# Scores on 128 contraction rows and five single-column fp32 products in a two-block transformer kernel

## The reference

```
block 1: h = rms_norm(x);  u = h @ w_in  ->  lru_x, lru_g, q, k, v      (8 heads of 64)
         y = [ rms_norm(gelu(lru_g) * rg_lru(conv(lru_x))),
               rms_norm(stick_breaking_attention(q, k, v)) ]
         x = x + y @ w_out;   x = x + (silu(g) * u) @ w_ffn_out,  [g, u] = rms_norm(x) @ w_ffn_in
         x = rms_norm(x)
block 2: proj = rms_norm(x) @ w_in_2  ->  cb, cc, cin, q, k, v, f, gates
         y_conv = (cb * causal_dwconv(cc * cin)) @ w_out_conv
         y_attn = forgetting_attention(q, k, v, log_sigmoid(f)) @ w_out_attn
         x = x + (g_conv * y_conv + g_attn * y_attn) @ w_o
         x = x + (silu(a) * b) @ w_down,  [a, b] = causal_dwconv(rms_norm(x) @ w_up);   rms_norm(x)
```

## Time and profile before

| what | value |
|---|---|
| time, median of 3 | 1388.01 us (1386.06 to 1389.28) |
| the profiled execution's own time | 1387.45 us |
| its span, first to last instruction | 1385.7 us |
| mean granted clock of TensorE, share of full speed | 0.990 |
| busy PE / PEld | 1352.9 us / 1079.1 us |
| busy DVE / ACT / POOL | 778.6 / 510.6 / 93.7 us |
| first attention, from its first scores to its last values | 126.9 to 219.6 us |
| second attention | 874.4 to 945.2 us |

### The profile page before, as it was taken

The page is one execution under the profiler, slowest core; times in us unless marked ns, Lnnn a source line. Parts: engine busy times, 40 slices in busy tenths (PEclk is TensorE's granted clock), DMA queues, the critical chain, the costliest instruction groups (busy, mean ns, idle before and its releaser), DMA issues.

```text
span 1385.7 us, 15739 instructions
## 1 busy us (share of the span) xinstructions
PE 1352.9 (98%) x6278; PEld 1079.1 (78%) x6278; DVE 778.6 (56%) x885; ACT 510.6 (37%) x575; POOL 93.7 (7%) x82
## 2 busy tenths in 40 slices
PE   7999999999999999997999999999999999999997
PEld 5777567788888889995888888657888888888886
DVE  6796644844433367876436433455666667674232
ACT  5463553332121235554211322444343344342122
POOL 4001010300000011224000000000310000000000
PEclk9999899999999999999999999999999999999999
DMA  4322000132233349651342222200323232233231
GB/s 163 122 92 91 31 0 31 61 122 91 91 96 104 132 124 257 124 102 56 126 149 91 92 91 93 90 1 31 109 74 121 69 113 91 91 104 109 63 105 61
DMA packets 103348, 130.35 MB, mean 94 GB/s; under 512 B 3338, under 2 KB 80378, under 8 KB 103170
## 3 DMA queue, kind: packets, MB, share of 16 engines
q1 hardware_dynamic: 97282, 115.99, 25.5%
q0 software_dynamic: 6000, 13.65, 5.1%
q10 hardware_dynamic: 16, 0.00, 0.0%
HBM read 127.52 MB, written 2.11 MB: 94 GB/s over the span
## 4 chain that ended last, share of the span: by engine, by line
PE 91%; issue 3%; DVE 2%; POOL 2%; ACT 1%; DMA 0%; ACTq 0%; SPq 0%; POOLq 0%; DVEq 0%
PE psum L1485 26%; PE psum L1486 26%; PE psum L1487 25%; PE psum L1607 3%; PE psum L1631 2%; PE psum L1619 2%; PE psum L1810 2%; DVE w_lo L906 1%; POOL tmp L557 1%; PE psum L1756 1%; PE psum L1758 1%; PE psum L1757 1%; ACT w_hi L588 1%; PE psum L1822 1%; DMA xin<-in_x 0%
## 5 line engine op out<-in xcount | busy, mean ns | idle before, releaser
L1485 PE MATMUL psum<-act_hi,w_hi 128*128 128x512 f32 x1224 | 485.8, 397 | 13.2 <-DVE act_lo L915 6.5
L1486 PE MATMUL psum<-act_lo,w_hi 128*128 128x512 f32 x1224 | 482.5, 394 | 0.0
L1487 PE MATMUL psum<-act_hi,w_lo 128*128 128x512 f32 x1224 | 481.7, 394 | 0.0
L588 ACT ACTIVATE w_hi<-raw 128x2048 fp32r<-128x2048 f32 (+1 forms) x102 | 192.5, 1887 | 594.8 <-PE psum L1487 583.6
L906 DVE TENSOR_TENSOR w_lo<-raw,w_hi 128x2048 fp32r<-128x2048 f32 (+1 forms) x102 | 233.7, 2291 | 127.1 <-ACT w_hi L588 127.1
L1485 PEld LDWEIGHTS psum<-act_hi,w_hi 128*128 128x128 f32 x1224 | 230.8, 189 | 73.0 <-issue 12.4
L1486 PEld LDWEIGHTS psum<-act_lo,w_hi 128*128 128x128 f32 x1224 | 231.0, 189 | 51.7 <-issue 1.4
L1487 PEld LDWEIGHTS psum<-act_hi,w_lo 128*128 128x128 f32 x1224 | 230.8, 189 | 50.5
L1756 PE MATMUL psum<-part_hi,w_hi 128*128 128x256 f32 x308 | 86.3, 280 | 1.8 <-DVE w_lo L906 1.8
L1758 PE MATMUL psum<-part_hi,w_lo 128*128 128x256 f32 x308 | 85.6, 278 | 0.0
L1757 PE MATMUL psum<-part_lo,w_hi 128*128 128x256 f32 x308 | 85.6, 278 | 0.0
(11 more groups left out here) (250 smaller groups left out, 1518.8 us busy)
## 6 DMA issues: line engine op xcount, KB each, us to landing
raw<-in_w_in SPq DMA_DIRECT2D x30, 1024.0 KB, 5.1
raw<-in_w_ffn_in SPq DMA_DIRECT2D x22, 1024.0 KB, 5.1
raw<-in_w_up SPq DMA_DIRECT2D x22, 1024.0 KB, 5.0
raw<-in_w_down SPq DMA_DIRECT2D x10, 1024.0 KB, 5.0
x_buf<-in_w_ffn_out POOLq DMA_DIRECT2D x6, 1024.0 KB, 10.5
raw<-in_w_out SPq DMA_DIRECT2D x4, 1024.0 KB, 5.0
raw<-in_w_o SPq DMA_DIRECT2D x4, 1024.0 KB, 5.2
x_buf<-in_w_ffn_out POOLq DMA_DIRECT2D x3, 768.0 KB, 10.9
```

Of the source, the lines that this page charges most:

```text
L588: A(w_hi[:, s % 2, 0:n], home(s, n), ACT.Copy).then_inc(w_hi_ready, 1)
L1485: mm(dst, stationary[0], moving[0], start=first, stop=False)
L1486: mm(dst, stationary[0], moving[1], start=False, stop=False)
L1487: return mm(dst, stationary[1], moving[0], start=False, stop=last)
```

## The change

The first part is in the scores. The keys of an odd head are copied by POOL from `kT[64:128, c]` to a new buffer `k_odd`, whose partitions 0 to 63 are set to zero, and then `kT[64:128, c]` is set to zero. So `kT` holds even heads over zeros and `k_odd` zeros over odd heads, and both are multiplied with all 128 rows of `qT`. In the second block the queries are treated so (`q_odd` has three places; its fourth chunk waits until heads 0 and 1 have their scores). The buffer `yatt` is gone: the output of the first attention is written over `qT`. TensorE waits for the padded chunk before the scores of each even head.

The second part is `one_column(bank)`: the fp32 identity times its own first column into an unused bank of the slab's half, whose result nobody reads. It stands ahead of `S_CC`, of `S_O2` and `S_O2 + 1`, and of the first slab of each feed-forward.

```diff
@@ POOL, after the sums of each group of norms
+                if rs[0] == N_LRU:
+                    pool.wait_ge(sq_summed, n)
+                    g.memset(k_odd[0:HD], 0.0).then_inc(pad_zeroed, 1)
+                    pool.wait_ge(pad_zeroed, 1)
+                    for c in range(WC):
+                        pool.wait_ge(evicted, K_EVICTED + c // 2)
+                        if c:
+                            pool.wait_ge(k_padded, c)
+                        g.tensor_copy(k_odd[HD:P, c], kT[HD:P, c]).then_inc(odd_copied, 1)
+                        pool.wait_ge(odd_copied, c + 1)
+                        g.memset(kT[HD:P, c], 0.0).then_inc(k_padded, 1)
+                    pool.wait_ge(k_padded, WC)
+                if rs[0] == N_FINAL:
+                    pool.wait_ge(slab_done, S_GA)
+                    pool.wait_ge(sq_summed, n)
+                    g.memset(q_odd[0:HD], 0.0).then_inc(q_pad_zeroed, 1)
...
+                        if c == WC - 1:
+                            pool.wait_ge(s_done, 2 * 3)
+                        g.tensor_copy(q_odd[HD:P, c % 3], q2[HD:P, c]).then_inc(q_odd_copied, 1)
+                        pool.wait_ge(q_odd_copied, c + 1)
+                        g.memset(q2[HD:P, c], 0.0).then_inc(q_padded, 1)
@@ DVE, att_out (ACT's att_operand and both split_act likewise)
-                V.tensor_copy(yatt[:, c], psum[:, 0]).then_inc(src_ready, 1)
+                V.tensor_copy(qT[:, c], psum[:, 0]).then_inc(src_ready, 1)
@@ PE
+            def one_column(bank):
+                mm(psum[:, bank, 0:1], ident[:], ident[:, 0:1], start=True, stop=True)
...
             def scores_kq(h):
+                if h % 2 == 0:
+                    pe.wait_ge(k_padded, h // 2 + 1)
+                keys, both = (k_odd if h % 2 else kT)[:, h // 2], qT[:, h // 2]
...
-                    mm(dst, head_rows(kT, h, kb * P, P), head_rows(qT, h, kb * P, n), start=kb != 3, stop=False,
+                    mm(dst, keys[:, kb * P:(kb + 1) * P], both[:, kb * P:TOKENS], start=kb != 3, stop=False,
...
             def up(s0, q, r):
                 wait_banks(GROUP[s0])
+                one_column(bank_of(GROUP[s0]) + 2)
                 slab_a(s0, q=q)
...
+                if s == S_CC:
+                    one_column(bank_of(GROUP[s]) + 2)
...
+                if s in (S_O2, S_O2 + 1):
+                    wait_freed(GROUP[S_OA2])
+                    one_column(bank_of(GROUP[s]) + 2)
```

More of the change, by code:

```diff
@@ L214, in freed @@
     return "evicted", 1 + EVICTED_BEFORE[g]
+K_EVICTED = 1 + EVICTED_BEFORE[GROUP[S_K]]
 C_MIX, C_LRU, C_ATT, C_FFN, C_MIX2, C_Z2, C_O2, C_M2, C_UP2 = 0, 8, 12, 16, 24, 32, 36, 40, 48
@@ L289, in two_blocks @@
         v = sb("v", [P, TB, WIDTH], F32, scope)
-        yatt = sb("yatt", [P, WC, TOKENS], F32, scope)
+        k_odd = sb("k_odd", [P, WC, TOKENS], F32, scope)
         gate_bd = sb("gate_bd", [P, 2, WC, P], F32, inner)
@@ L325, in two_blocks @@
         probs = sb("probs", [P, 2, CAUSAL], F32, inner)
+        q_odd = sb("q_odd", [P, 3, TOKENS], F32, inner)
         probs_T = tmp[:, 0:5].rearrange("p a n -> p (a n)").rearrange("p (a n) -> p a n", a=2)
@@ L381, in two_blocks @@
         f_abs = sem("f_abs")
+        pad_zeroed, odd_copied, k_padded = sem("pad_zeroed"), sem("odd_copied"), sem("k_padded")
+        q_pad_zeroed, q_odd_copied, q_padded = sem("q_pad_zeroed"), sem("q_odd_copied"), sem("q_padded")
         ms2_ready, f_pre, f_exp, f_ln, f_sum = sem("ms2_ready"), sem("f_pre"), sem("f_exp"), sem("f_ln"), sem("f_sum")
@@ L566, in _ @@
                     g.dma_start(neg_f[:].rearrange("p h n -> p (h n)"), every).then_inc(negf_in, 16)
+                if rs[0] == N_LRU:
[14 more added lines that the diff above has]
+                    g.memset(q_odd[0:HD], 0.0).then_inc(q_pad_zeroed, 1)
+                    pool.wait_ge(q_pad_zeroed, 1)
+                    for c in range(WC):
+                        if c:
+                            pool.wait_ge(q_padded, c)
+                        if c == WC - 1:
[3 more added lines that the diff above has]
+                        g.memset(q2[HD:P, c], 0.0).then_inc(q_padded, 1)
+                    pool.wait_ge(q_padded, WC)
                 if rs[0] == N_MIX:
@@ L667, in att_operand @@
                 act.wait_ge(src_ready, C_ATT + c + 1)
-                square(yatt[:, c])
-                split_act(C_ATT + c, act_hi[:, WC + c], yatt[:, c], col("norm_att_out", c), S_V + 2)
+                square(qT[:, c])
+                split_act(C_ATT + c, act_hi[:, WC + c], qT[:, c], col("norm_att_out", c), S_V + 2)
             def weights(h):
@@ L1093, in _ @@
                     c = (h - 4) // 2
-                    split_act(C_ATT + c, act_hi[:, WC + c], act_lo[:, WC + c], yatt[:, c], col("norm_att_out", c))
+                    split_act(C_ATT + c, act_hi[:, WC + c], act_lo[:, WC + c], qT[:, c], col("norm_att_out", c))
             att_out(WC - 1)
             c = WC - 2
-            split_act(C_ATT + c, act_hi[:, WC + c], act_lo[:, WC + c], yatt[:, c], col("norm_att_out", c))
-            split_act(C_ATT + WC - 1, act_hi[:, DC - 1], act_lo[:, DC - 1], yatt[:, WC - 1], col("norm_att_out", WC - 1))
+            split_act(C_ATT + c, act_hi[:, WC + c], act_lo[:, WC + c], qT[:, c], col("norm_att_out", c))
+            split_act(C_ATT + WC - 1, act_hi[:, DC - 1], act_lo[:, DC - 1], qT[:, WC - 1], col("norm_att_out", WC - 1))
             for s in (S_OUT_LRU, S_OUT_LRU + 1):
@@ L1596, in columns @@
                 return psum[:, head_bank(h) + at // TOKENS, at % TOKENS:at % TOKENS + n]
-            def head_rows(x, h, t0, n):
-                p = HD * (h % 2)
-                return x[p:p + HD, h // 2, t0:t0 + n]
             def values(h, weights, v_rows, bank):
@@ L1803, in scores_qk @@
             def scores_qk(h):
+                c = h // 2
+                if h % 2 == 0:
+                    pe.wait_ge(q_padded, c + 1)
+                queries = q_odd[:, c % 3] if h % 2 else q2[:, c]
                 for i in QUERY_ORDER:
@@ L1809, in scores_qk @@
                     dst = columns(h, QUERY_AT[i], n)
-                    mm(dst, head_rows(q2, h, i * P, P), head_rows(k2, h, 0, n), start=i != 0, stop=False,
+                    mm(dst, queries[:, i * P:(i + 1) * P], k2[:, c, 0:n], start=i != 0, stop=False,
                        skip_group_check=True)
```

## The result

The changed kernel takes **1362.76 us** (median of 4, 1362.08 to 1363.01), the kernel before on the same chip 1387.6 us (median of 4, 1386.06 to 1389.28): ratio 0.982 with a 95% interval of 0.9803 to 0.9837. The profiled execution took 1362.54 us (span 1360.8, mean granted clock 0.997), where the prediction's sum said 1363.7 for it and 1364.3 for the median.

The account below looks back on a forecast made before the run. TensorE's stream (PE busy 98% of the span) was taken to bound the kernel; -13.6 + 1.2 - 8.0 - 3.4 = -23.8 from 1387.45 us gave 1363.7, with the median's 0.56 about 1364.3 us; range 1359 to 1378.

Parts of the forecast that it names:

- The scores: Both attentions: with 128 rows throughout, a head's scores take 2.65 us instead of 3.49; 16 heads give -13.6 us.
- The rival by which the format would keep the mask's load exposed: Scores: fp32 ahead of bf16 breaks the flow, only 7.6 us gained instead of 13.6; 1370.3 us, chance 0.17.
- The waits: Second attention: TensorE waits for DVE's normalising of head 1 and briefly in later even heads, +1.2 us.
- The one that was named: Second attention: the transposes of head 1 wait once for DVE's normalising, 0.9 us.
- three later small waits: Second attention: later even heads may wait about 0.1 us each, three times.
- The clock: Attentions: full rows keep the clock up, giving back half the low-clock time, 8.5 us, taken as -8.0.
- The three stretches: Clock at the lower level with PE busy, at 152.13, 162.37 and 892.90: 3.42, 6.83 and 6.70 us.
- The columns: Dense products: faster pace from `S_CC` and `S_O2` on, -4.2 us, less 0.9 paid for five columns: -3.4 us.
- the step: From `S_O2` to the first slab of `up(S_UP)`: 240 products at the faster pace, 4.4 ns each, 1.05 us gained.
- POOL: Copies and memsets for padding cost nothing: first chunk ready near 122.5, scores at 126.91, cover 4 us.
- The prediction's warning that a stretch could come out at the longer pace: Rival: one or both feed-forward loops come out at 233 ns, 1368.7 to 1373.1 us, chance 0.12.

Follow-up runs that it names:

- the 64-row kernel: The kernel before, its scores on 64 rows as they were and the masks put on 64 rows too: 1368.58 us, ratio 0.9865.
- the second look at the rows alone: The changed kernel without its five single columns, run once more for its profile: 1365.27 us (one run).

## Why the prediction was right, and where it was right by luck

**The scores** (-13.6). The head of 2.65 us is met to the hundredth where it stands behind the values. Behind a piece of `w_out` it is 183.87 - 181.32 = 2.55, since the first load is hidden there too, and the pause ahead of the head is shorter (0.23 us from the last product of `w_out`, 0.32 before). From one such head to the next it is 190.57 - 181.32 = 9.25 us in the changed kernel and 192.47 - 182.19 = 10.28 before, 1.03 less. The timeline of PE, first in the changed kernel, then in the kernel before:

```profile
181.32 0.81 PE L1655 MATMUL psum<-qT,kT 128*128 128x384 f32 x2
...
183.87 0.55 PE L1667 MATMUL psum<-soft,neg_ones 128*128 128x128 f32 x3
...
190.57 0.81 PE L1655 MATMUL psum<-qT,k_odd 128*128 128x384 f32 x2
```

```profile
182.19 0.91 PE L1619 MATMUL psum<-qT,kT 64*128 64x384 f32 x2
...
192.47 0.91 PE L1619 MATMUL psum<-qT,kT 64*128 64x384 f32 x2
```

The prediction gave every head the same gain: 3.49 - 2.65 is 0.84, which it rounded to 0.85. With the steps as measured, and 0.84 for the three heads in which the clock fell before, the sixteen heads gain about 14.6 us, 1.0 more than its term.

The mechanism is shown, not only its size: 64-row scores with 64-row masks lose the gaps, 128-row scores with 64-row masks have them again, with equal formats. The rival by which the format would keep the mask's load exposed is out. The Trainium skill ("TensorE: Matmul & The Clock Gate", "Part 3: Packing small matmuls — row/col tiling") states in its list of what overlaps that a load overlaps running products only across different row groups; beside that, the same section lets loads into a background weight buffer go ahead. The runs here speak against the first as a general rule: between products of equal rows, 64 or 128, and 128 stationary columns the load is hidden (0.06 us from a mask to the next block), and it is exposed where the number of rows changes (0.16 us). Equal rows alone are not enough: behind the values, of 128 rows and 64 columns, 0.1 us of the head's first load stays exposed, as the prediction had it.

**The waits** (+1.2). The one that was named is there, in two pieces. First the last mask and the transposes of head 1 in the timeline of PE, then the loads of the last two of these transposes (PEld), then the first and the last part that DVE normalises for that head (the answer to the earlier trace rows).

```profile
875.84 0.22 PE L1855 MATMUL psum<-mask_qk,ident_bf 128*128 128x128 bf16 x1
876.54 1.73 PE L1865 MATMUL psum<-ident,probs 128*128 128x128 f32 x10 [0.48 <-DVE probs L1375]
```

```profile
877.83 0.20 PEld L1865 LDWEIGHTS psum<-ident,probs 128*128 128x128 f32 x2 [0.32 <-DVE probs L1375]
```

```profile
875.91 0.48 DVE L1375 TENSOR_SCALAR probs<-probs,small 128x512 f32<-128x512 f32 x1
...
877.42 0.35 DVE L1375 TENSOR_SCALAR probs<-probs,small 128x256 f32<-128x256 f32 x1
```

The transposes start at 876.54, behind the first part (875.91 + 0.48 = 876.39); the last two go on at 877.83, behind the last part (877.42 + 0.35 = 877.77). A product that waits for nothing comes 0.06 us after the start of a mask and 0.11 after that of a transpose. So 0.64 us are lost ahead of the first transpose and 0.35 between the eighth and the ninth, 1.0 in all where 0.9 was said. The prediction let the transposes wait once, for the last part; they wait for each part as it comes. Of the three later small waits two are there, in heads 3 and 5 (counted from 0, so odd and not even ones): from the first transpose to the values it is 1.28 us there and 1.19 in heads 2 and 6. They are too short for the list of waits. Together that is the 1.2 us of the prediction.

**The clock** (-8.0). The three stretches are gone. The attentions together lost 21.2 us, where the terms of scores, waits and clock made 20.4. With 14.6 for the scores and 1.2 for the waits, 7.8 are left for the clock; the changed kernel with its masks on 64 rows gave 6.9 + 1.4 = 8.3 for the same term. What the runs add: the rows of the scores decide. With 64 rows and gaps the clock fell three times (before, and the columns alone), with 64 rows and no gaps once, with 128 rows and gaps never, with 128 rows and none never. These are counts from one profile each, but the mean granted clock over a whole execution, which is known for each timed one, goes the same way: 0.988 to 0.993 in 35 of 36 executions of the kernel before (0.996 in one) and 0.989 to 0.995 in twelve with the columns alone; 0.994 to 0.996 in four with 64 rows and no gaps; 0.995 to 0.998 in seven with 128 rows and gaps; 0.996 to 0.999 in 23 with 128 rows and none. That gaps count beside the rows is less sure, since only four executions have 64 rows without them. Half of the 128 rows are zeros in the stationary operand, so the zeros didn't bring the clock down; whether scores of 128 rows without zeros would keep it as well was not run. What exactly makes it fall is not settled.

**The columns** (-3.4). Behind `S_CC` 3.1 us came where 3.2 less 0.2 was said. All eight profiles with a column at that place (the changed kernel and seven experiments) have the shorter pace; of the four without, three have the longer (before, the 64-row kernel, the second look at the rows alone) and one the shorter. The column makes sure of what is otherwise chance. One thing about this chance the profiles do show. The products of `S_V2` have the weights as their moving operand, and in all twelve profiles they run at 233.3 ns, from their first products on; so do those of `w_down`. Here is the stretch of `S_V2` in the kernel before:

```profile
682.00:703.00 21.00, 21.00 (x91) 16.83 (x90) 7.45 (x7) 6.36 (x6) 1.16 (x2) 1.00 0.70 246
```

So `S_CC` always starts behind a stretch at the longer pace. Without a column it kept that pace in three profiles of four, and with one it never did. That no column turned `S_V2` or `w_down` themselves fits this; why the moving operand matters was not tested.

By their times alone the padded kernels can't be told apart: ratio 0.9831 (0.9812 to 0.985) without columns, 0.9827 (0.9801 to 0.9854) with one, 0.982 (0.9803 to 0.9837) with five. What the columns are worth is read from the stretches, and from the kernel before with the columns alone, 0.9981 (0.9968 to 0.9994).

At `S_O2` the step failed, though its sum came out. The prediction said -1.05 and some 0.6 for the columns, and the stretch behind the second attention gave -0.41; but all four other profiles without columns there (the two looks at the rows alone, the 64-row kernel, the one with the column of `S_CC` alone) have the shorter pace as well, and end in 439.73 or 439.74 us behind the second attention. The longer pace at 964 was one execution's, and the columns there only cost their 0.6 us. The reasoning "behind an fp32 product it came out fast more often than slow" took a chance event for a rule, as the columns at more places then showed.

**POOL** (0). The timeline of POOL in the changed kernel, and that of PE for the first scores, the answers to the earlier trace rows.

```profile
117.92 1.81 POOL L576 MEMSET k_odd<- 64x2048 f32 x1
119.79 0.69 POOL L582 COPY k_odd<-kT 64x512 f32<-64x512 f32 x1
120.54 0.52 POOL L584 MEMSET kT<- 64x512 f32 x1
...
124.50 0.52 POOL L584 MEMSET kT<- 64x512 f32 x1
```

```profile
126.05 0.81 PE L1655 MATMUL psum<-qT,kT 128*128 128x384 f32 x2
```

The first chunk is ready at 120.54 + 0.52 = 121.06, 1.4 us earlier than said (copies of 0.6 to 0.7 us on 64 partitions, not 1.29), and all four before the first scores. The cover for the first is 5 us.

**What no term held.** The seven products of 256 columns took 0.8 us more, six of them at 117.8 ns instead of four, and the start 0.86 less. The one is a chance of pace (the kernel with the rows alone had five at 117.8 in one execution and six in the other), the other lies in the first transfers and products, which the change doesn't touch; they cancel. The prediction's warning that a stretch could come out at the longer pace was right for these.

## What to carry to other kernels

Look at the distances between starts, not at busy shares: a TensorE that is 98% busy lost 25 us of 1388 to uncovered loads, a lower clock and a longer pace. Where small products alternate, try the same number of rows in all of them, even if half are zeros: here the change of rows alone cost 14.3 us. A list of waits leaves out the short ones; a third of the wait for head 1 shows only in the distances between its transposes. A cheap trick whose mechanism is unknown is to be looked at without it, and more than once, since one profile shows one outcome of a chance.

## What the runs showed of the hardware

- A change between 64 and 128 rows costs some 0.1 us on either side of a bf16 mask between fp32 passes; the change from fp32 to bf16 and back costs no such gap. Heads behind the values take 3.49 and 3.58 us with the change of rows, 2.65 and 2.74 without.
- TensorE, with hardly a pause, fell to a granted clock of 0.50 three times in the attentions with 64-row fp32 scores (16.95 us in all, in the profile of the kernel before) and kept 1.00 in the same scores padded to 128 rows, with and without gaps between the passes.
- Dense products of 512 columns have two paces, 228.9 and 233.3 ns (of 256 columns 113.3 and 117.8), which hold over hundreds of products; where nothing else stood in between they were seen to change only at borders of slabs. `S_V2` and `w_down`, whose moving operand is the weights, had 233.3 in all twelve profiles; elsewhere one kernel showed both at the same place in two executions. An fp32 column ahead of `S_CC` always led to the shorter, ahead of the products of 256 columns, `S_V2` and `w_down` never. What sets the pace stays open.
